# Two steps of a product-key expert layer put in another order: VectorE's step in V begins with the next tile's weights, ScalarE's step in U with the high part two tiles on

## The chip, the core and the metric

The kernel runs on one core of one Trainium2 chip. The metric is the time of one execution on the device in microseconds (us). Three executions before the change gave 3698.55, 3700.45 and 3706.06 us; their median is 3700.45 us.

## What is computed

The reference is a trunk of two layers for 512 tokens of width 1024, all in float32. Each layer has a gated mixer (attention and a convolution) and then an expert retrieval, which alone the change touches. Cut to that part:

```
q = (xt @ w_query).reshape(T, 8, 2, 128)
s = einsum('thpd,hpnd->thpn', q, sub_keys)      # scores against 2 x 128 half keys
... top 16 of each half, top 16 of their sums: ids, gates = softmax(top_s)
a    = gelu(einsum('chkd,cd->chk', u_tab[idc], xc))   # u_e . x of each chosen expert
coef = gc * a
y    = einsum('chk,chkd->cd', coef, v_tab[idc])       # sum of coef * v_e
```

There are 128 x 128 = 16384 experts in each layer, and `u_tab` and `v_tab` have a row of 1024 for each.

## The kernel before

The kernel doesn't gather the experts' rows for 384 of the 512 tokens. It multiplies the whole tables on TensorE, and weights the result with a matrix that is zero where an expert was not chosen. Only the first 128 tokens get their rows one by one: GpSimd gathers 128 rows of 4 KB at a time (`gbuf`, four buffers), and VectorE multiplies them.

**Tiles.** All matrices come as one stream of 340 tiles for each layer, each 128 x 1024 float32 (512 KB), into four slots, `raw[:, i % 4]`. The stages in order are the mixer's projections (tiles 0 to 67), the queries (68 to 83), **U** (tiles 84 to 211, the table `u`) and **V** (212 to 339, the table `v`). SyncE's queue loads tile i + 4 into a slot when TensorE has finished tile i (`load`, which waits for `tile_done`).

**The split.** Each tile is used as three products. In U and V the steps to make them ready are:
- `high_at` (U) and `high_in` (V), on ScalarE: the high part `w_hi` from `raw` (lines 1000 and 1007, "HI" below). It waits for the load alone.
- `u_low` (U, line 1715) and `weight_low` (V, line 1934), on VectorE: the 16-bit remainder `w16[.., 0]`, from `raw` and `w_hi` ("WL"). It is written into the slot of `raw`.
- `half_word`, on ScalarE (line 1012, "HW"): the 16-bit copy of the high part, `w16[.., 1]`. It is written over the rest of `raw`, so that it waits for WL of its tile.

**TensorE in a tile.** `product16` (U) and `experts` (V) first wait for HI and run 8 float32 products (lines 667 and 924), then wait for HW and run 16 products of 16-bit operands (lines 670, 671, 927 and 928).

**U, the other work.** After tile u ScalarE applies gelu to the bank (line 1256) and stores the 384 columns to `g_scr`. Between tiles 33 and 117, 48 groups build the gates' matrix: VectorE makes `one_j`, `one_i`, `gated_hi` and `gated_lo` (lines 1894 to 1899), TensorE multiplies them (lines 895 and 897, `c_group`), ScalarE copies the result to `stage` (line 1288), and SyncE's queue stores it to `c_scr`. VectorE's `dot` (line 1740) takes a gathered row block in between. The order on ScalarE in one U tile is HW(u+1), HI(u+2), gelu(u).

**V, the other work.** The right-hand side of tile k is made by `mix(k)` on VectorE (lines 1921 and 1922, "MX", from `cg`, which SyncE's queue loads from the two scratch arrays), `coef_high(k)` on ScalarE (lines 1264 and 1265, "CH"), and `mixed_low(k)` on VectorE (line 1928, "ML"), which waits for CH. `weigh(k)` (line 1913, "WG") adds one gathered row block of `v` to `y_sp`, and lets GpSimd gather the next. TensorE waits for ML(k) and HI(k) before tile k. ScalarE runs, in one V tile, CH(k+1), HW(k+1), HI(k+2). Every eighth step VectorE also takes a row of the next conditioning product (`w_row`, line 1354). VectorE's loop has 32 steps in one turn, with 3 turns and 32 further steps written out; TensorE's and ScalarE's have 4 tiles in one turn.

The waits are written by hand as semaphore counts, and each engine runs its instructions in the order of the program.

Of the kernel before, what the change touches and what calls it, by code (L numbers as in the profile page):

```python
# [79 lines left out]
I_U = 84  # L80
# [91 lines left out]
def build_trunk(nc, stream, u_rows, ada, params_d, keys_d, con_d, x_d, c_d, pos_d, c_scr, g_scr, out_d):  # L172
    with ExitStack() as ctx:
# [792 lines left out]
        def _(act):  # L966
# [25 lines left out]
            with act.Fori(0, DEPTH) as l:  # L992
                def read_no(i):

                    return l * (NE // 2) + i // 2 + 2

                def high_at(i):
                    act.wait_ge(loaded[i % 4], (l * (NT // 4) + i // 4 + 1) * 16)
                    if I_QRY <= i < NT:
                        nc.scalar.mul(w_hi[:, i % 4], raw[:, i % 4], W_UP).then_inc(hi_done, 1)  # L1000
                    else:
                        nc.scalar.copy(w_hi[:, i % 4], raw[:, i % 4]).then_inc(hi_done, 1)
# [6 lines left out]
                def half_word(s, g):  # L1009

                    act.wait_ge(lo_done, g + 5)
                    nc.scalar.mul(w16[:, s, 1], w_hi[:, s].bitcast(F32), X_DOWN).then_inc(w16_done, 1)  # L1012

                def half_word_at(i):

                    half_word(i % 4, l * NT + i)
# [66 lines left out]
                for i in range(I_Q + C):  # L1083
# [10 lines left out]
                    else:  # L1094
                        k = i - I_K if i < I_V else i - I_Q + 2
# [152 lines left out]

                def u_tile(u):

                    half_word_at(I_U + u + 1)
                    high_at(I_U + u + 2)
                    b = u % 2
                    act.wait_ge(g_st[b], (l * (NKEYS // 2) + u // 2) * 16 + 16)
                    act.wait_ge(tile_done, l * NT + I_U + u + 5)
                    nc.scalar.activation(g_out[:, b], ps[:, b, 0:ND], ACT.Gelu).then_inc(bank_read[b], 1)
                    act.wait_ge(bank_read[b], read_no(I_U + u))
                    act.dma_start(g_scr[u], g_out[:, b]).then_inc(g_st[b], 16)
# [8 lines left out]
                u = 0  # L1267
                while u < EXP_TILE:
                    u_tile(u)
                    u += 1  # L1270
                act.wait_ge(g_exp, 2 * l + 1)
                nc.scalar.activation(t16[:], t16[:], ACT.Exp).then_inc(g_exp, 1)
                while u < U_ROUTE:
                    u_tile(u)
                    u += 1
                g = 0
                while u < NKEYS:
                    if u == NKEYS - 1:
                        coef_high(0, 0)
                    u_tile(u)  # L1280
                    while g < GROUPS and group_tile(g) == u:
                        hb = g // HALF_GROUPS
                        if g % HALF_GROUPS == 0:
                            act.wait_ge(c_st, (l * STORED + max(hb - 1, 0)) * 16 * PARTS + 64)
                        for q in range(2):
                            n, tok = 2 * g + q, (GROUP * g + 4 * q) % HALF
                            act.wait_ge(c_mm, l * 2 * GROUPS + n + 5)
                            nc.scalar.mul(stage[:, hb % 2, :, tok:tok + 4].rearrange("i j t -> i t j"),
                                          ps[:, 2 + n % 4].rearrange("i (t j) -> i t j", t=4), X_UP / GATE_UP).then_inc(c_ev, 1)
                        g += 1  # L1290
                        if g == GROUPS:
                            nc.scalar.copy(st[:, 0, 4], st[:, 0, 3]).then_inc(cg_free, 4)
                    u += 1
# [26 lines left out]
        def _(dve):  # L1320
# [85 lines left out]
            with dve.Fori(0, DEPTH) as l:  # L1406
# [501 lines left out]
                def weigh(k, r):  # L1908

                    at_k = dve.snap(4 * r + k)  # L1910
                    dve.wait_ge(row_in[k % 4], (l * (2 * P // SLOTS) + P // SLOTS + r + k // 4 + 1) * 16)
                    dve.wait_ge(row_used, l * 2 * P + P + 4 * r + k + 4)
                    nc.vector.scalar_tensor_tensor(out=y_sp[:], in0=gbuf[:, k % 4], scalar=a_sp[:, bass.ds(at_k, 1)],  # L1913
                                                   in1=y_sp[:], op0=ALU.mult, op1=ALU.add).then_inc(row_used, 1)

                def mix(k, r):

                    dve.wait_ge(cf_ready, l * NKEYS + 4 * r + k + 3)
                    dve.wait_ge(cg_in[k % 4], (l * (NKEYS // 4) + r + k // 4) * 32 + 32)
                    j = dve.snap(4 * r + k)  # L1920
                    nc.vector.tensor_tensor(coef[:, k % 2, 0:NS], cg[:, k % 4, 0:NS], cg[:, k % 4, NS:2 * NS], ALU.mult)
                    nc.vector.tensor_tensor(coef[:, k % 2, NS:].rearrange("i (b t) -> i b t", b=2), stage[:, :, bass.ds(j, 1)].rearrange("i b o t -> i (b o) t"),
                                            cg[:, k % 4, 2 * NS:].rearrange("i (b t) -> i b t", b=2), ALU.mult).then_inc(cg_free, 1)

                def mixed_low(k, r):

                    dve.wait_ge(cf_hid, l * NKEYS + 4 * r + k + 1)
                    nc.vector.scalar_tensor_tensor(out=cf16[k % 4][:, 0], in0=cf_hi[k % 4][:].bitcast(F32), scalar=-1.0 / X_DOWN,  # L1928
                                                   in1=coef[:, k % 2], op0=ALU.mult, op1=ALU.add).then_inc(cf_ready, 1)

                def weight_low(k, r):

                    dve.wait_ge(hi_done, l * NT + I_W + 4 * r + k + 1)
                    nc.vector.scalar_tensor_tensor(out=w16[:, k % 4, 0], in0=raw[:, k % 4], scalar=W_UP,  # L1934
                                                   in1=w_hi[:, k % 4].bitcast(F32), op0=ALU.mult,
                                                   op1=ALU.subtract).then_inc(lo_done, 1)

                def w_step(k, r, left=2):

                    if left >= 2:  # L1940
                        mix(k + 2, r)
                    weigh(k, r)
                    if left >= 1:
                        mixed_low(k + 1, r)
                        weight_low(k + 1, r)

                mix(0, 0)
                mix(1, 0)
# [22 lines left out]
                with dve.Fori(0, 3) as r:  # L1971
                    for k in range(32):
                        w_step(k, 8 * r)
                        if k % 8 == 5:
                            w_row(k // 8, r)
                    w_rows_kept(r)
                for k in range(32):
                    w_step(k, 24, 31 - k)
                    if k % 8 == 5:
                        w_row(k // 8, 3)  # L1980
# [81 lines left out]
```

## Time and profile before

| | before |
|---|---|
| three executions | 3698.55, 3700.45, 3706.06 us |
| the profiled execution | 3699.43 us |
| its span | 3697.6 us |
| TensorE matmul busy | 3378.1 us (91%) |
| VectorE busy | 2995.0 us (81%) |
| ScalarE busy | 2179.2 us (59%) |
| GpSimd busy | 1029.0 us (28%) |
| moved by DMA | 868.89 MB, mean 235 GB/s |

The span is what the profile covers from the first to the last instruction; the execution is 1.8 us longer. V takes about 1255 to 1843 us in the first layer and 3095 to 3685 us in the second, U about 640 to 1250 and 2480 to 3090 us. A busy share says how long an engine held an instruction, not whether it set the pace; for that the waits and the timeline are read.

### The profile page before, as it was taken

The numbers are of one execution on the slowest core, as the hardware profiler recorded it, in microseconds if no ns is written. First come the engines' busy times: TensorE is split into PE (matmuls) and PEld (weight loads), VectorE is DVE, ScalarE is ACT, GpSimd is POOL, SyncE is SP. The second block draws the span as 40 slices with busy tenths as digits, with TensorE's granted clock in tenths as the row PEclk, the third lists the DMA queues.
The fourth block names the chain that finished last, engine by engine and source line by source line (L and its number), as shares of the span: only waits on it lengthen the run. The fifth ranks groups of instructions, "written<-read, shape, count | busy, mean of one in ns | idle before, by whom it ended". The sixth has DMA issues, their size and how long they took to land.

```text
span 3697.6 us, 63120 instructions
## 1 busy us (share of the span) xinstructions
PE 3378.1 (91%) x19278; PEld 2439.2 (66%) x19278; DVE 2995.0 (81%) x6039; ACT 2179.2 (59%) x3118; POOL 1029.0 (28%) x1126
## 2 busy tenths in 40 slices
PE   6999999989999998899989999999899988988998
PEld 5767766666666666666677677666666666666665
DVE  6999769987788677777769997799877786777777
ACT  4573445566776565566646724455677765655666
POOL 0000036035555322222200000550445552222221
PEclk9999999999999999999999999999999999999999
DMA  5312353579998999999822124435799989999997
GB/s 194 98 58 80 127 203 112 188 233 327 332 351 297 328 320 298 304 311 311 283 80 87 58 86 166 170 122 192 258 331 340 340 294 337 309 308 296 318 307 246
DMA packets 421669, 868.89 MB, mean 235 GB/s; under 512 B 167824, under 2 KB 233360, under 8 KB 421008
## 3 DMA queue, kind: packets, MB, share of 16 engines
q1 hardware_dynamic: 310512, 544.87, 43.8%
q0 software_dynamic: 73728, 268.47, 21.6%
q10 hardware_dynamic: 37152, 52.45, 3.8%
q8 instruction: 102, 1.67, 0.2%
q14 instruction: 175, 1.43, 0.1%
HBM read 774.41 MB, written 85.98 MB: 233 GB/s over the span
## 4 chain that ended last, share of the span: by engine, by line
issue 59%; POOL 14%; DVE 11%; ACT 10%; PE 3%; DMA 1%; ACTq 1%; DVEq 1%; POOLq 0%; SPq 0%
DVE w L1934 6%; POOL gbuf L586 5%; ACT w_hi L1007 5%; POOL spare L600 4%; ACT cf_hi L1265 2%; POOL raw L559 2%; ACT cf L1264 2%; POOL w L562 2%; DVE y_sp L1913 1%; DVE w_rows L1354 1%; PE ps L667 1%; DMA gbuf<-u_rows,ids_u 1%; PE ps L670 1%; PE ps L671 1%; POOL h L575 1%
## 5 line engine op out<-in xcount | busy, mean ns | idle before, releaser
L1012 ACT ACTIVATE w<-w_hi 128x1024 f16<-128x1024 f32 x544 | 574.8, 1057 | 776.8 <-DVE w L1934 472.3
L670 PE MATMUL ps<-h,w 128*128 128x384 f16 (+1 forms) x2272 | 756.6, 334 | 20.8 <-ACT w L1012 20.7
L927 PE MATMUL ps<-cf,w 128*128 128x384 f16 x2032 | 666.7, 329 | 100.3 <-ACT w L1012 100.2
L671 PE MATMUL ps<-h,w 128*128 128x384 f16 (+1 forms) x2272 | 753.3, 332 | 0.0
L928 PE MATMUL ps<-cf,w 128*128 128x384 f16 x2032 | 663.4, 327 | 0.0
L600 POOL TENSOR_TENSOR spare<-spare 128x1 f32<-128x1 f32 x504 | 218.5, 434 | 1400.0 <-DVE y_sp L1913 814.3
L667 PE MATMUL ps<-h_hi,w_hi 128*128 128x384 f32 (+1 forms) x2272 | 491.0, 358 | 0.0
L924 PE MATMUL ps<-cf_hi,w_hi 128*128 128x384 f32 x2032 | 435.4, 357 | 27.4 <-DVE cf L1928 27.0
L1715 DVE SCALAR_TENSOR_TENSOR w<-raw,w_hi 128x1024 f16<-128x1024 f32 x248 | 302.6, 1220 | 185.4 <-ACT w_hi L1000 185.2
L667 PEld LDWEIGHTS ps<-h_hi,w_hi 128*128 128x128 f32 x2272 | 396.9, 189 | 17.3 <-issue 0.2
L927 PEld LDWEIGHTS ps<-cf,w 128*128 128x128 f16 x2032 | 199.4, 98 | 295.5 <-ACT w L1012 176.1
L924 PEld LDWEIGHTS ps<-cf_hi,w_hi 128*128 128x128 f32 x2032 | 359.2, 191 | 46.9 <-issue 30.1
L670 PEld LDWEIGHTS ps<-h,w 128*128 128x128 f16 x2272 | 222.7, 98 | 214.1 <-issue 42.0
L1928 DVE SCALAR_TENSOR_TENSOR cf<-cf_hi,coef 128x384 f16<-128x384 f32 x256 | 142.8, 558 | 257.3 <-ACT cf_hi L1265 256.7
L586 POOL DMA_INDIRECT gbuf<-u_rows,ids_u x256 | 338.3, 1321 | 41.9 <-POOL spare L600 13.1
L1506 DVE SCALAR_TENSOR_TENSOR yT<-uT,lp,yT 128x512 f32<-128x512 f32 x480 | 327.4, 744 | 0.0
L1913 DVE SCALAR_TENSOR_TENSOR y_sp<-gbuf,a_sp,y_sp 128x1024 f32<-128x1024 f32 x256 | 327.0, 1277 | 0.0
L671 PEld LDWEIGHTS ps<-h,w 128*128 128x128 f16 x2272 | 223.9, 99 | 140.2 <-issue 1.7
L1740 DVE CUSTOM_DVE_ANT_1 gbuf<-gbuf,h_tok 128x1024 f32<-128x1024 f32 x256 | 303.3, 1219 | 15.9 <-DMA gbuf<-u_rows,ids_u 15.7
L1000 ACT ACTIVATE w_hi<-raw 128x1024 fp32r<-128x1024 f32 x296 | 309.5, 1046 | 11.3 <-DMA raw<-stream 10.8
L1934 DVE SCALAR_TENSOR_TENSOR w<-raw,w_hi 128x1024 f16<-128x1024 f32 x256 | 311.7, 1218 | 0.0
L586 POOL DMA_INDIRECT gbuf<-stream,ids_v x256 | 273.2, 1067 | 38.8 <-issue 3.1
(286 smaller groups left out, 6152.2 us busy)
## 6 DMA issues: line engine op xcount, KB each, us to landing
raw<-stream SPq DMA_DIRECT2D x682, 512.0 KB, 5.0
gelu_scratch<-g_out ACTq DMA_DIRECT2D x256, 192.0 KB, 6.7
cg<-gelu_scratch SPq DMA_DIRECT2D x256, 192.0 KB, 5.5
c_scratch<-stage SPq DMA_DIRECT2D x128, 256.0 KB
cg<-c_scratch SPq DMA_DIRECT2D x256, 128.0 KB, 4.3
qT<-ada SPq DMA_DIRECT2D x32, 512.0 KB, 6.5
cgate<-ada SPq DMA_DIRECT2D x32, 512.0 KB, 5.7
w_rows<-ada SPq DMA_DIRECT2D x32, 512.0 KB, 7.2
```

Source lines behind the costliest of these rows:

```text
L586: nc.gpsimd.indirect_dma_start(out=gbuf[:, n % SLOTS], out_offset=None, in_=table, in_offset=bass.IndirectOffsetOnAxis(ap=ids[:, k:k + 1], ...
L600: nc.gpsimd.tensor_tensor(spare[:, 16:17], spare[:, 17:18], spare[:, 18:19], ALU.add).then_inc(room, 1)
L667: nc.tensor.matmul(ps[:, b, 0:n], w_hi[:, s, c], h_hi[:, c, t0:T], start=c == 0, stop=False)
L670: nc.tensor.matmul(ps[:, b, 0:n], w16[:, s, 0, c], h16[:, c, 1, t0:T], start=False, stop=False)
L671: mm = nc.tensor.matmul(ps[:, b, 0:n], w16[:, s, 1, c], h16[:, c, 0, t0:T], start=False, stop=c == C - 1)
L924: nc.tensor.matmul(ps[:, c, P:T], w_hi[:, s, c], cf_hi[s][:], start=first, stop=False)
L927: nc.tensor.matmul(ps[:, c, P:T], w16[:, s, 0, c], cf16[s][:, 1], start=False, stop=False)
L928: mm = nc.tensor.matmul(ps[:, c, P:T], w16[:, s, 1, c], cf16[s][:, 0], start=False, stop=False)
L1012: nc.scalar.mul(w16[:, s, 1], w_hi[:, s].bitcast(F32), X_DOWN).then_inc(w16_done, 1)
L1506: ins = nc.vector.scalar_tensor_tensor(out=yT[:, c], in0=uT[:, c, k:k + T], scalar=weight, in1=yT[:, c], op0=ALU.mult, op1=ALU.add)
L1913: nc.vector.scalar_tensor_tensor(out=y_sp[:], in0=gbuf[:, k % 4], scalar=a_sp[:, bass.ds(at_k, 1)], in1=y_sp[:], op0=ALU.mult, op1=ALU.add ...
L1934: nc.vector.scalar_tensor_tensor(out=w16[:, k % 4, 0], in0=raw[:, k % 4], scalar=W_UP, in1=w_hi[:, k % 4].bitcast(F32), op0=ALU.mult, op1= ...
```

## The change

In U, ScalarE takes HI(u+2) first and HW(u+1) behind it. In V, VectorE's step k ran MX(k+2), WG(k), ML(k+1), WL(k+1); now it runs WL(k+1), ML(k+1), MX(k+2), WG(k). No instruction is added or removed, and no wait's count is changed.

```
                 def u_tile(u):

+                    high_at(I_U + u + 2)
                     half_word_at(I_U + u + 1)
-                    high_at(I_U + u + 2)
                     b = u % 2
...
                 def w_step(k, r, left=2):

+                    if left >= 1:
+                        weight_low(k + 1, r)
+                        mixed_low(k + 1, r)
                     if left >= 2:
                         mix(k + 2, r)
                     weigh(k, r)
-                    if left >= 1:
-                        mixed_low(k + 1, r)
-                        weight_low(k + 1, r)
```

## Rows read from the trace of the kernel before

**Rows 1.** Waits of the whole run: engine, line, waited for: us, times, longest

```profile
ACT w L1012 <- DVE w L1934: 472.3, 256, 6.3
...
DVE cf L1928 <- ACT cf_hi L1265: 256.7, 220, 3.3
DVE w L1715 <- ACT w_hi L1000: 185.2, 98, 3.2
...
PE ps L927 <- ACT w L1012: 100.2, 236, 0.5
...
PE ps L895 <- DVE gated_lo L1899: 66.3, 61, 2.1
...
PE ps L924 <- DVE cf L1928: 27.0, 8, 4.5
...
PE ps L670 <- ACT w L1012: 20.7, 25, 2.4
...
ACT w_hi L1000 <- DMA raw<-stream: 10.8, 14, 1.6
```

**Rows 2.** Timeline, one tile of V: start us, us, engine line op [idle before]

```profile
1504.20 0.42 DVE L1921 TENSOR_TENSOR coef<-cg 128x256 f32<-128x256 f32 x1
1504.32 1.06 ACT L1012 ACTIVATE w<-w_hi 128x1024 f16<-128x1024 f32 x1 [1.76 <-DVE w L1934]
...
1504.54 0.28 DVE L1922 TENSOR_TENSOR coef<-stage,cg 128x128 f32<-128x128 f32 x1
1504.74 1.28 DVE L1913 SCALAR_TENSOR_TENSOR y_sp<-gbuf,a_sp,y_sp 128x1024 f32<-128x1024 f32 x1
...
1505.28 1.04 ACT L1007 ACTIVATE w_hi<-raw 128x1024 fp32r<-128x1024 f32 x1
...
1505.43 0.34 PE L927 MATMUL ps<-cf,w 128*128 128x384 f16 x1 [0.42 <-ACT w L1012]
...
1506.23 0.51 ACT L1264 ACTIVATE cf<-coef 128x384 f16<-128x384 f32 x1
...
1506.64 0.51 ACT L1265 ACTIVATE cf_hi<-coef 128x384 fp32r<-128x384 f32 x1
...
1507.18 0.56 DVE L1928 SCALAR_TENSOR_TENSOR cf<-cf_hi,coef 128x384 f16<-128x384 f32 x1 [1.16 <-ACT cf_hi L1265]
...
1507.66 1.22 DVE L1934 SCALAR_TENSOR_TENSOR w<-raw,w_hi 128x1024 f16<-128x1024 f32 x1
...
1507.91 1.69 PE L924 MATMUL ps<-cf_hi,w_hi 128*128 128x384 f32 x8
...
1508.91 1.06 ACT L1012 ACTIVATE w<-w_hi 128x1024 f16<-128x1024 f32 x1 [1.76 <-DVE w L1934]
```

**Rows 3.** Timeline of TensorE in V just after VectorE's loop turned

```profile
1573.88 1.69 PE L924 MATMUL ps<-cf_hi,w_hi 128*128 128x384 f32 x8
...
1577.88 1.69 PE L924 MATMUL ps<-cf_hi,w_hi 128*128 128x384 f32 x8
```

**Rows 4.** DMA issues of the page: KB each, median us from issue to landing

```profile
raw<-stream SPq DMA_DIRECT2D x682, 512.0 KB, 5.0
```

**Rows 5.** Windows: busy us of each engine, TensorE clock, DMA share, GB/s

```profile
1000.00:1060.00 60.00, 57.01 (x407) 40.88 (x404) 49.64 (x74) 45.02 (x52) 29.90 (x30) 1.00 0.99 349
...
1417.00:1550.00 133.00, 121.59 (x699) 84.39 (x698) 102.68 (x152) 82.08 (x116) 37.61 (x59) 0.99 0.94 306
...
3100.00:3220.00 120.00, 108.94 (x629) 75.50 (x629) 93.19 (x139) 73.91 (x105) 33.27 (x52) 1.00 0.97 326
```

**Rows 6.** Timeline of VectorE where its loop turns in V

```profile
1413.61 0.42 DVE L1921 TENSOR_TENSOR coef<-cg 128x256 f32<-128x256 f32 x1 [5.41 <-issue]
```

**Rows 7.** Timeline of ScalarE in U, one tile

```profile
807.99 1.06 ACT L1012 ACTIVATE w<-w_hi 128x1024 f16<-128x1024 f32 x1 [1.76 <-DVE w L1715]
808.95 1.04 ACT L1000 ACTIVATE w_hi<-raw 128x1024 fp32r<-128x1024 f32 x1
```

**Rows 8.** Timeline of VectorE in U, the same place

```profile
810.03 1.23 DVE L1715 SCALAR_TENSOR_TENSOR w<-raw,w_hi 128x1024 f16<-128x1024 f32 x1 [2.07 <-ACT w_hi L1000]
```

## The prediction, made before the changed kernel was run

> **What bounds the kernel now.** I read the waits first. Two of ScalarE's and VectorE's waits stand out, and they face each other: HW in V waits 472.3 us for WL, in 256 of 256 tiles, and ML waits 256.7 us for CH, which is ScalarE's [rows 1]. Two engines that wait for each other in every tile are a ring, whatever their busy shares. So the next view is the timeline of one V tile, and the reader should follow it as a circle [rows 2]. HW starts at 1504.32, HI 0.96 us later, the first half of CH 0.95 later, the second 0.41 later; ML starts 0.54 later, WL 0.48 later, and 1.25 after that, at 1508.91, the next HW. The sum is 0.96 + 0.95 + 0.41 + 0.54 + 0.48 + 1.25 = 4.59 us. That is the whole period: nothing in it is a wait for TensorE or a DMA. TensorE's first 16-bit product waits for HW [rows 2], 236 times in V [rows 1].
>
> How fast TensorE would be alone is seen where it had a backlog, behind a turn of VectorE's loop: there the tiles start 4.00 us apart [rows 3]. So 0.59 us of each 4.59 is the ring's. The 0.42 us that the waits show (100.2 us in all [rows 1]) understates it, since the ends of matmuls are modelled.
>
> In U the chain is another. ScalarE's HW waits for WL, HI stands behind HW, and VectorE's next WL waits for HI: 2.07 us at 810.03 [rows 8], 98 times and 185.2 us in all [rows 1]. The gates' operands come behind that WL, and TensorE waits for them 61 times, 66.3 us, and for HW 25 times, 20.7 us [rows 1]. That is 87 us in both layers.
>
> **V, part by part.** Nothing is added. The VectorE operations of a step keep their durations: from start to start 0.48 (ML), 0.34 and 0.20 (MX), and WL and WG last 1.22 and 1.28 [rows 2], together 3.52 us. ScalarE's four take 0.96 + 0.95 + 0.41 + 0.51 = 2.83 us. Both are below TensorE's 4.00, also with a conditioning row every eighth step. What changes is who waits. WL(k+1) no longer stands behind ML(k+1), so not behind CH(k+1) either. It needs HI(k+1) alone, which ScalarE finished in the step before. The ring is cut, and three shorter ones are left:
> - WL, HW, HI of the next tile, WL: 1.25 + 0.96 + 1.07 = 3.28 us for a tile.
> - CH, ML, MX of the next tile, CH: 0.92 + 0.03 + 0.48 + 0.34 + 0.31 = 2.08 us.
> - HI, WL, ML, MX, WG, WL, HW, HI over two tiles: 1.07 + 1.22 + 0.48 + 0.54 + 1.28 + 1.25 + 0.96 = 6.80 us, 3.4 for one.
>
> ML(k+1) behind WL(k+1) costs nothing: CH takes 0.92 us after HI, WL 1.25, so CH is done first. Moved back are MX(k+2) and WG(k). MX has SyncE's queue behind it, which loads the coefficients for four tiles on and then waits for TensorE's tile anyway; WG has GpSimd behind it, whose gather is wanted four tiles later. Their cover is the four buffers, 4 x 4 us against a landing of 5.0 us for a load of the stream [rows 4]. If that cover went, each would cost its lateness once in a tile. The raw slots have the same cover: from the end of tile k to the start of k+4 are three tiles, 12 us, for the landing and HI.
>
> So something else bounds the tile: TensorE at 4.00, or the DMA engines. They are busy 0.94 of V at 306 GB/s, 0.97 at 326 in the fuller stretch [rows 5]. A tile moves 306 x 4.59 = 1.41 MB. Estimates of its least time: if packets keep their lengths and the share can reach the 0.99 seen in U, 4.59 x 0.94 / 0.99 = 4.36 us. If V can have U's 349 GB/s [rows 5], 1.41 MB take 4.03 us. The packets get shorter under load, as the rows show: 306 / 0.94 is 326 GB/s for a full share, 326 / 0.97 is 336, and U's 349 / 0.99 is 353. I take V's own fuller stretch, 336 GB/s, and get 1.41 / 336 = 4.20 us, since U moves fewer short pieces and is the farther row. The gain is 0.39 us in each of the 236 tiles that waited [rows 1]: 92 us. The ends are 0.23 x 236 = 54 and 0.59 x 236 = 139.
>
> At this place a page of the Trainium skill says more, and my sum doesn't use it. "DMA: Bandwidth & Descriptors", section "Where 436 GB/s comes from", puts the limit from HBM at about 358 GB/s for a core. By that rule 1.41 MB would take 3.94 us, TensorE would be the bound, and the gain would be the 139 us end. The trace agrees so far as no window of these rows is above it (349), but V's share is nearly full at 306 to 326.
>
> **The turns of the loop.** VectorE stands 5.41 us at a turn for its instructions [rows 6]; TensorE waits for ML 8 times, 27.0 us in all, at the turns and at V's start [rows 1]. After the change VectorE can be ahead when it stops: it needs only HI, thus the load, which lands about a tile before its need. I take 8 of the 27 us; the ends are 0, if the DMAs take up the lead, and 27.
>
> **U.** HI(u+2) goes ahead of HW(u+1). At 807.99 ScalarE had been idle for 1.76 us when HW began, and HI came at 808.95 [rows 7]: HI could begin up to 2.7 us earlier if its load has landed, and VectorE's 2.07 us of waiting [rows 8] go, with the group's operands behind. HW(u+1) comes up to 1 us later, where ScalarE isn't idle; it is covered by TensorE's tile in hand, as HW is made a tile ahead. Behind it are gelu(u), its store and the group's copy, each of which waits for TensorE's tile u. Not covered is a late load: HW(u+1) now waits for the load of tile u+2, and ends up to 1.04 + 1.06 = 2.1 us after it lands [rows 7]. That happens where HI waits for its load today, 14 times in U and the queries, 10.8 us [rows 1], so at most 14 x 2.1 = 29 us lost. The ends for U are thus 29 us lost and 87 gained. I take 30 gained: half of the 87, since part of those waits is VectorE's own work in tiles with a group each and part a late load, less half of the 29.
>
> **The sum.** 92 + 8 + 30 = 130 us. The profiled execution took 3699.4 us (span 3697.6 and 1.8 around it), so 3569.4; the median of the runs is 1.0 above it. I predict 3570 us.
>
> **Rivals, and their chances.**
> - My forecast, DMA engines and TensorE nearly level, 3530 to 3610: 0.42.
> - The DMA engines bound V by their time, 4.36 us for a tile. For it: a share of 0.94 to 0.97 [rows 5]. Against: packets that shorten under load. 54 us in V, none at the turns, 15 in U: 3631. Chance 0.18.
> - TensorE bounds V at 4.00. For it: four tiles' cover, and U's 349 GB/s. 139 + 16 + 40 = 195 us: 3504. Chance 0.17. This is also where the page's 358 GB/s would lead.
> - V as forecast, but U loses, because faster tiles make loads late and HW is held behind HI in as many places as today's 14: 100 - 29 = 71 us, 3629. Chance 0.12.
> - The change doesn't do in V what it says: another ring of the same length closes, for example CH(k+1) behind HI(k+1) with ML and MX behind it, or a gather that lands late because WG moved back. Against it stand the three sums above, the longest 3.4 us. Only U's 30 us stay: 3669. Chance 0.07.
> - Slower: in U ScalarE is held at loads in most tiles, 2.1 us each. It decides from 100 / 2.1 = 48 of the 256 U tiles on; at 96 tiles the time is 3699 - 100 + 202 = 3801. For it: U's share of 0.99 in the densest window. Against: 14 late loads now. Chance 0.04.
>
> About 0.2% (7 us) is what a measurement of this kernel can tell from no change. Faster by more than that are all but the last two cases and most of the last but one, 0.93; 0.03 within, where V keeps its pace and U gives nothing; 0.04 slower. The range that leaves out no more than 2 in 10 reaches from the TensorE case to just past the DMA case: 3500 to 3645.
>
> **What would show it.** ML's wait for CH and HW's wait for WL in V nearly gone; the order on VectorE WL, ML, MX, WG, and HW no longer 0.03 us behind WL. Tile starts of line 924 about 4.2 us apart instead of 4.59; if 4.0, TensorE bounds, and if 4.36 or uneven, with HI waiting for `raw`, the DMA engines do. The DMA share in V at 0.97 or more and 336 GB/s. In U, WL's wait for HI well below 185 us, the wait for `gated_lo` about halved, and some new waits of line 670 for HW behind HI's wait for a load. My prediction is wrong above all if V's packets don't shorten, or if they shorten as in U.

## The result, and the profile after

The changed kernel took 3491.93 us (median of 4, 3484.96 to 3496.24), beside 3700.9 us before: a ratio of 0.9432, 95% interval 0.941 to 0.9453. That is 209 us less, where 130 were forecast, and below the range of 3500 to 3645. The direction, the ring and the place of the gain were right. The size was not: the case that the prediction gave 0.17 came in, TensorE as the bound of V (3504), with more from U on top.

Where the time went is read from the starts of TensorE's tiles in the two profiled executions, whose spans differ by 203 us (3697.6 and 3494.4). From the first to the last tile of V it took 1194.0 us in both layers together before and 1040.8 after, 153 less. From the first to the last tile of U it was 1228.4 and 1177.6, 51 less. (The first layer's V before reaches to 1858.6 us, not to 1843 as said above.)

First the waits of the changed kernel, whole run (engine, line, waited for: us, times, longest). They answer to [rows 1].

```profile
ACT w L1012 <- DVE w L1934: 174.5, 254, 5.5
ACT w_hi L1007 <- DMA raw<-stream: 125.2, 114, 3.7
DVE w L1934 <- ACT w_hi L1007: 113.6, 106, 3.3
...
ACT w_hi L1000 <- DMA raw<-stream: 105.5, 96, 3.5
...
DVE w L1715 <- ACT w_hi L1000: 97.3, 60, 4.5
...
PE ps L670 <- ACT w L1012: 40.0, 36, 3.1
...
PE ps L924 <- DVE cf L1928: 23.6, 9, 4.3
...
DVE cf L1928 <- ACT cf_hi L1265: 6.3, 2, 3.2
```

The two lines that closed the ring are changed: HW's wait for WL fell from 472.3 to 174.5 us, and ML's for CH from 256.7 us, 220 times, to 6.3 us, 2 times. TensorE's wait for HW in V (line 927, 100.2 us before) is gone. In its place a wait appears that V did not have: HI waits for its load, 114 times. In U and the queries the same wait went from 14 times to 96. ScalarE now stands at the loads, which costs nothing as long as TensorE has a tile in hand. One sign that the prediction named did not come: HW still waits for WL 254 times, and starts 0.03 us behind its end in the tile shown next, since ScalarE gets to HW before WL has ended. That wait no longer sets the period.

One tile of V on the timeline (start us, us, engine, line), to be laid beside [rows 2]:

```profile
1444.23 1.69 PE L924 MATMUL ps<-cf_hi,w_hi 128*128 128x384 f32 x8
1444.50 1.06 ACT L1007 ACTIVATE w_hi<-raw 128x1024 fp32r<-128x1024 f32 x1 [1.32 <-DMA raw<-stream]
1445.47 0.51 ACT L1264 ACTIVATE cf<-coef 128x384 f16<-128x384 f32 x1
1445.59 1.23 DVE L1934 SCALAR_TENSOR_TENSOR w<-raw,w_hi 128x1024 f16<-128x1024 f32 x1 [1.30 <-ACT w_hi L1007]
1445.88 0.51 ACT L1265 ACTIVATE cf_hi<-coef 128x384 fp32r<-128x384 f32 x1
1446.73 0.55 DVE L1928 SCALAR_TENSOR_TENSOR cf<-cf_hi,coef 128x384 f16<-128x384 f32 x1
1446.85 1.06 ACT L1012 ACTIVATE w<-w_hi 128x1024 f16<-128x1024 f32 x1 [0.47 <-DVE w L1934]
1447.20 0.42 DVE L1921 TENSOR_TENSOR coef<-cg 128x256 f32<-128x256 f32 x1
...
1448.23 1.69 PE L924 MATMUL ps<-cf_hi,w_hi 128*128 128x384 f32 x8
```

TensorE's tiles start 4.00 us apart (1444.23 and 1448.23), the pace that it showed only in its catch-up before [rows 3]. The next steps in V are 4.01 us for the most part. WL and CH now run side by side, WL on VectorE and CH on ScalarE, both from HI on; ML and HW follow at once. HW for the next tile ends at 1447.91, and TensorE's first product that needs it starts at 1449.76, about 1.5 us after the tile's start.

The windows of V (busy us of PE, PEld, DVE, ACT, POOL, then TensorE's clock, DMA share, GB/s):

```profile
1280.00:1350.00 70.00, 70.00 (x423) 50.11 (x420) 61.71 (x93) 50.11 (x69) 42.54 (x35) 1.00 1.04 365
1400.00:1470.00 70.00, 70.00 (x420) 50.38 (x419) 61.67 (x93) 51.54 (x72) 42.95 (x36) 1.00 1.05 360
1640.00:1740.00 100.00, 100.00 (x601) 71.80 (x600) 86.91 (x131) 71.71 (x100) 59.51 (x52) 1.00 1.02 347
```

Against [rows 5]: TensorE is busy 70.00 of 70 us at the full granted clock (2.4 GHz), and the DMAs move 347 to 365 GB/s; the two windows of V shown there had 306 and 326, and the same three stretches of the kernel before had 315, 298 and 319. The DMA share is 1.02 to 1.05: it is a sum of packets' times over 16 engines, and passes 1 here.

U, the groups' stretch of the first layer, waits of the changed kernel from 770 to 1240 us:

```profile
DVE w L1715 <- ACT w_hi L1000: 50.8, 30, 4.5
ACT w_hi L1000 <- DMA raw<-stream: 48.8, 45, 3.4
...
PE ps L670 <- ACT w L1012: 11.7, 10, 3.1
...
PEld ps L895 <- issue: 5.1, 10, 1.1
...
PE ps L895 <- DVE gated_lo L1899: 1.8, 3, 0.7
```

and the same lines and stretch of the kernel before:

```profile
DVE w L1715 <- ACT w_hi L1000: 88.1, 44, 3.1
PEld ps L895 <- issue: 49.2, 46, 2.5
PE ps L895 <- DVE gated_lo L1899: 32.4, 29, 2.1
...
ACT w_hi L1000 <- DMA raw<-stream: 3.1, 5, 0.9
PE ps L670 <- ACT w L1012: 2.0, 3, 0.9
```

TensorE's wait for the gates' operands went from 32.4 to 1.8 us, and the weight loads' idle time ahead of them from 49.2 to 5.1. Its wait for HW rose from 2.0 to 11.7: that is the cost of HW behind HI, and it is real but small. How much this makes for a tile is in the section on the prediction.

### The profile page after: what moved, and what is told of

It is laid out like the page before. It is cut to its first block, busy times and chain, and to the rows that moved or that the text cites. A ratio compares the mean times of both kernels' runs of the same rounds, so it can differ in the third digit from the quotient of the medians.

```text
span 3494.4 us, 63120 instructions
## 1 busy us (share of the span) xinstructions
PE 3328.6 (95%) x19278; PEld 2443.3 (70%) x19278; DVE 2984.3 (85%) x6039; ACT 2191.8 (63%) x3118; POOL 1330.3 (38%) x1126
## 4 chain that ended last, share of the span: by engine, by line
PE 40%; issue 26%; DVE 15%; POOL 10%; DMA 4%; ACT 3%; DVEq 0%; POOLq 0%; SPq 0%; ACTq 0%
PE ps L924 9%; PE ps L927 8%; PE ps L928 8%; POOL gbuf L586 6%; POOL spare L600 5%; PE ps L636 4%; PE ps L638 3%; PE ps L637 3%; DVE yT L1506 3%; DVE i L1752 2%; DMA raw<-stream 2%; DVE v L1748 1%; DVE S_ring L1758 1%; DMA gbuf<-u_rows,ids_u 1%; PE ps L670 1%
## 5 line engine op out<-in xcount | busy, mean ns | idle before, releaser
L1012 ACT ACTIVATE w<-w_hi 128x1024 f16<-128x1024 f32 x544 | 572.5, 1052 | 286.3 <-DVE w L1934 174.5
L600 POOL TENSOR_TENSOR spare<-spare 128x1 f32<-128x1 f32 x504 | 393.9, 782 | 909.2 <-DVE a_sp L1740 500.9
L924 PE MATMUL ps<-cf_hi,w_hi 128*128 128x384 f32 x2032 | 430.6, 354 | 23.6 <-DVE cf L1928 23.6
L1000 ACT ACTIVATE w_hi<-raw 128x1024 fp32r<-128x1024 f32 x296 | 313.7, 1060 | 144.6 <-DMA raw<-stream 105.5
L586 POOL DMA_INDIRECT gbuf<-stream,ids_v x256 | 383.3, 1497 | 38.3 <-POOL spare L600 2.6
L586 POOL DMA_INDIRECT gbuf<-u_rows,ids_u x256 | 352.7, 1378 | 40.9 <-POOL spare L600 9.5
L570 POOL TENSOR_TENSOR spare<-spare 128x1 f32<-128x1 f32 x2 | 0.4, 193 | 926.9 <-DVE w_lo L1411 926.9
L1007 ACT ACTIVATE w_hi<-raw 128x1024 fp32r<-128x1024 f32 x248 | 260.5, 1050 | 126.2 <-DMA raw<-stream 125.2
```

Source lines behind the costliest of these rows:

```text
L586: nc.gpsimd.indirect_dma_start(out=gbuf[:, n % SLOTS], out_offset=None, in_=table, in_offset=bass.IndirectOffsetOnAxis(ap=ids[:, k:k + 1], ...
L600: nc.gpsimd.tensor_tensor(spare[:, 16:17], spare[:, 17:18], spare[:, 18:19], ALU.add).then_inc(room, 1)
L924: nc.tensor.matmul(ps[:, c, P:T], w_hi[:, s, c], cf_hi[s][:], start=first, stop=False)
```

## The experiments

All ratios are to the kernel before, run on the same chip beside the changed one. Where a V order is tried in experiments 3 and 4, U has its new order.

**1. V's new order alone.** The edit is the second part of the diff; U is as before.

> V's new order alone, U as before. My theory after the result: the two parts are independent; in V the ring of 4.59 us is cut and TensorE's 4.01 us bounds each tile, about 146 us for both layers by the starts of the tiles, so about 3549 us. Rival: the U part also sets up V (DMAs further ahead at V's start), then V alone gives less, 3560 us or more.

Measured: 3551.33 us (3548.68 to 3554.53), ratio 0.9586 (0.957 to 0.9602), beside 3705.16: 154 us less. By the interval V's share of the gain is thus 147 to 159 us; by the tile starts V took 154 us less than before, and U 4 us more.

**2. U's new order alone.** The first part of the diff.

> U's new order alone, V as before. My theory: 51 us of the gain are U's, so about 3650 us, and V's tiles stay 4.59 us apart. Rival (my forecast's size): 30 us, 3670 us. Rival: HW held behind late loads takes the gain back, 3690 us or more.

Measured: 3638.61 us (3635.9 to 3646.66), ratio 0.9826 (0.9808 to 0.9844): 66.5 us less, 58 to 71 by the interval; by the tile starts U took 62 us less, and V the same as before. The expectation of 51 us was what the changed kernel's first profile showed in U; its repeat in experiment 9 shows 60, so U varies by some 10 us between executions. 30 and "taken back" are both refuted. The product of the two ratios is 0.9419, within the interval of the whole change, so the parts don't need each other.

**3. Only the last two change places.** WL ahead of ML, but both behind MX and WG.

```
                 def w_step(k, r, left=2):

                    if left >= 2:
                        mix(k + 2, r)
                    weigh(k, r)
                    if left >= 1:
-                        mixed_low(k + 1, r)
                         weight_low(k + 1, r)
+                        mixed_low(k + 1, r)
```

> The changed kernel, but V's step is MX, WG, WL, ML: of the old order only WL and ML change places, and nothing is moved ahead of MX and WG. Theory: what counts is that WL no longer stands behind ML and so behind CH; the ring is cut all the same, V's tiles 4.01 us apart, 3492 us within 10. Rival: WL must begin the step, since 1.8 us of MX and WG ahead of it make HW late; then tiles at 4.2 or more and 3540 us or more.

Measured: 3480.2 us (3474.85 to 3484.27), ratio 0.9397 (0.9381 to 0.9413), 2 us below the range expected. V's steps are 4.01 us and the rival of 3540 us is refuted: the whole of V's gain is in this one exchange.

**4. The pair first, ML still ahead of WL.**

```
                     if left >= 1:
-                        weight_low(k + 1, r)
                         mixed_low(k + 1, r)
+                        weight_low(k + 1, r)
                     if left >= 2:
                         mix(k + 2, r)
                     weigh(k, r)
```

> The changed kernel, but V's step is ML, WL, MX, WG: the pair begins the step, as in the change, but ML stays ahead of WL. Theory: the ring HW, HI, CH, ML, WL, HW is closed as before, each tile takes 4.59 us again, and only U's gain is left: 3640 to 3650 us. Rival: the gain is from taking the pair ahead of MX and WG; then 3500 us.

Measured: 3629.58 us (3626.64 to 3629.82), ratio 0.9794 (0.9778 to 0.981), 10 us below the range expected. The time is U's gain and 9 us more than in experiment 2. Those 9 us are mostly at the turns of VectorE's loop in V: TensorE's four steps from tile to tile over a turn took 8.46 to 9.45 us in experiment 2 and take 6.81 to 7.20 here, and V is 7.5 us shorter. The timeline of VectorE and ScalarE in V:

```profile
1450.00 1.06 ACT L1012 ACTIVATE w<-w_hi 128x1024 f16<-128x1024 f32 x1 [1.76 <-DVE w L1934]
...
1452.86 0.56 DVE L1928 SCALAR_TENSOR_TENSOR cf<-cf_hi,coef 128x384 f16<-128x384 f32 x1 [1.17 <-ACT cf_hi L1265]
1453.34 1.22 DVE L1934 SCALAR_TENSOR_TENSOR w<-raw,w_hi 128x1024 f16<-128x1024 f32 x1
...
1454.59 1.06 ACT L1012 ACTIVATE w<-w_hi 128x1024 f16<-128x1024 f32 x1 [1.76 <-DVE w L1934]
```

From HW to HW 4.59 us, with the same two waits as in [rows 2], 1.76 and 1.17. Taking the pair to the head of the step does nothing for the tile, and is worth some 8 us at the turns; putting WL ahead of ML is what cuts the ring. Experiments 3 and 4 together show it.

**5. The kernel before with less for TensorE.** In 127 of the 128 V tiles of a layer 8 of 24 products are left out (the last tile has lines of its own; the expectations say 125), so the output lacks them.

```
                     for c in W_ORDER:
-                        nc.tensor.matmul(ps[:, c, P:T], w16[:, s, 0, c], cf16[s][:, 1], start=False, stop=False)
                         mm = nc.tensor.matmul(ps[:, c, P:T], w16[:, s, 1, c], cf16[s][:, 0], start=False, stop=False)
```

> The kernel before with the same 8 products of a V tile left out. Theory: the ring of ScalarE and VectorE sets the tile, so its 4.59 us stay although TensorE has 1.3 us less to do, and the time stays within 10 us of before. Rival: TensorE is part of the pace; then tiles fall below 4.4 us and the kernel gains 50 us or more.

Measured: 3703.12 us, one run, beside 3703.72. Some 330 us less work for TensorE (8 products of 0.16 us in 254 tiles) changed nothing. Its timeline of TensorE:

```profile
1451.28 1.66 PE L924 MATMUL ps<-cf_hi,w_hi 128*128 128x384 f32 x8 [0.97 <-DVE cf L1927]
...
1455.87 1.66 PE L924 MATMUL ps<-cf_hi,w_hi 128*128 128x384 f32 x8 [0.97 <-DVE cf L1927]
```

The tiles are still 4.59 us apart, now with a wait of 0.97 us ahead of them.

**6. The changed kernel with the same products left out.** The same edit.

> The changed kernel with 8 of the 24 products of a V tile left out (the 8 of the 16-bit remainder with cf16[.., 1]; 125 of 128 tiles). Its output lacks them. TensorE's tile falls from 4.01 to 2.7 us, so that what comes next is seen. Theory: the DMA engines can do more than my forecast gave them; the tile comes down to VectorE's own 3.4 to 3.6 us, with 390 GB/s or more. Rival: DMAs stood just below the surface at the 352 to 362 GB/s of the changed kernel; then tiles stay at 3.9 to 4.0 us.

Measured: 3451.64 us, one run: 28 to 40 us below the changed kernel's two medians (3479 and 3492), of the same 330 us. So something stands close beneath TensorE. From 1280 to 1350 us 18 tiles are loaded, 3.9 us each, at 373 GB/s (the third window behind experiment 8), and VectorE is busy 61.91 of 70 us. The starts of the tiles tell the two apart. Of the 254 steps 127 are at most 3.45 us, most of them 3.34 us, which is VectorE's own step (3.35 us from one WL to the next behind the turn shown below). The others are longer: 4.48 us where VectorE takes a conditioning row as well, and up to 5.7 us elsewhere (7.9 at the turns); the mean is 3.96 us. ScalarE waits for loads there, 78 times and 93.0 us in V. So VectorE sets about half of these tiles, and late loads are what is seen to wait in the rest.

**7 and 8. The changed kernel with more bytes.** Behind each load of V from the fifth tile on, a half (7) or a quarter (8) of the next tile is loaded once more, to a place that nobody reads. The edit for a half, without the buffers and semaphores that it needs:

```
                         load(k % 4, l * NT + I_W + 32 * r + k + 4)
+                        if k >= 4 or k0 == 0:
+                            n = sp.snap(l * NT + I_W + 32 * r + k + 4)
+                            sp.wait_ge(more_in[k % 4], (l * 30 + 8 * r + k // 4) * 16)
+                            sp.dma_start(more[k % 4][:], stream[n][:, 0:C // 2]).then_inc(more_in[k % 4], 16)
```

> The changed kernel with 256 KB more loaded beside each V tile from the fifth on (a half of the next tile once more, into a free place that nobody reads). A tile then moves 1.67 MB instead of 1.41. Theory: the limit of the DMA engines is near 390 GB/s, so tiles of 4.2 to 4.3 us, 50 to 70 us more than the changed kernel. Rival 1 (my forecast's 336 to 353 GB/s hold for long): 4.7 to 5.0 us. Rival 2 (the limit is above 415 GB/s): the tile stays 4.01 us.

> As with 256 KB more beside each V tile, but 128 KB. The two runs before put the limit of the DMA engines in V at 364 to 372 GB/s, whatever the tile held. Theory: a tile of 1.573 MB then takes 4.2 to 4.3 us where the conditioning rows are loaded, and 1.507 MB 4.05 to 4.15 us in the last quarter; 3530 to 3550 us in all. Rival: there is no fixed limit, a tile slows with each added transfer in proportion (0.7 us for 256 KB), so 4.35 us in all quarters.

Measured: 3614.56 us with 256 KB and 3538.07 us with 128 KB, one run each. The larger one is 0.49 us a tile more than the changed kernel (118 us between the profiled spans of 3612.7 and 3494.4, over about 240 tiles), not the 0.2 to 0.3 expected, nor the 0.7 to 1.0 of the forecast's rates. With that limit known, the smaller one came within its range, and its tiles roughly too: from quarter to quarter of V, without the first two steps of each, 4.24, 4.24, 4.28 and 4.11 us in the first layer, 4.37, 4.32, 4.22 and 4.15 in the second; the last quarter has no conditioning rows. The rival, 4.35 us in all quarters, doesn't fit. The windows from 1280 to 1350 us, in this order: with 256 KB, with 128 KB, and the changed kernel with fewer products:

```profile
1280.00:1350.00 70.00, 62.98 (x366) 43.30 (x365) 55.67 (x84) 45.89 (x64) 26.60 (x30) 1.00 1.06 376
```

```profile
1280.00:1350.00 70.00, 67.52 (x396) 46.60 (x394) 55.26 (x83) 45.88 (x64) 27.56 (x32) 1.00 1.07 372
```

```profile
1280.00:1350.00 70.00, 54.40 (x279) 36.83 (x277) 61.91 (x93) 50.80 (x71) 43.68 (x37) 0.95 1.07 373
```

Three kernels with different tiles end at the same 372 to 376 GB/s. (In the last quarter of V, from 1640 to 1700 us, it is 358, 370 and 365.) And in the one with 256 KB more the waits of this window are:

```profile
ACT w_hi L1014 <- DMA raw<-stream: 18.7, 12, 3.4
...
PE ps L931 <- DVE cf L1938: 7.0, 7, 2.5
```

HI waits for loads again (line 1014 there), and now TensorE waits too, which in the changed kernel it did not. That is what a bound by DMA looks like here, about 373 GB/s in V. Whether the DMA engines or the memory behind them set it, no run here shows. It holds for V's mix of transfers alone: in U the changed kernel moved more for 12 us,

```profile
1036.00:1048.00 12.00, 10.11 (x70) 7.23 (x68) 7.34 (x12) 6.48 (x8) 6.94 (x8) 1.00 1.03 389
```

**9 and 10. The changed kernel again, beside the order of experiment 3.**

> The changed kernel once more, beside the next one on the same chip: 3480 to 3496 us, ratio about 0.943 to before.

> The order MX, WG, WL, ML in V once more. Its first run was 0.9397 of before, the changed kernel's 0.9432. Theory: both stand at TensorE's 4.01 us in V and have the same U, so within 0.2% of each other here. Rival: MX and WG early let the transfers behind them start early, which is worth 5 to 12 us.

Measured, five executions each: the change 3479.09 us (3472.91 to 3481.09), ratio 0.938 (0.9366 to 0.9394); the order MX, WG, WL, ML 3486.98 us (3481.89 to 3489.03), ratio 0.9401 (0.9388 to 0.9414). The lead of experiment 3 over the first measurement of the change did not hold. Here the change is ahead by 8 us, 0.2%, there it was behind, and the intervals overlap; neither order is shown to be the better. The expectation for the change itself, 0.943, was missed by half a per cent: its ratio moved by as much from one measurement to the other.

## Why the prediction was wrong, step by step

- **The ring.** Right. 0.96 + 0.95 + 0.41 + 0.54 + 0.48 + 1.25 is the period of 4.59 us, TensorE has no part in it (experiment 5), and WL ahead of ML cuts it (3 and 4). It held for nearly all of V's tiles, not only for the 236 that the prediction counted by TensorE's waits: 227 of the 254 steps from tile to tile are 4.59 us before, and 237 are 4.01 after.
- **TensorE's own pace, 4.00 us, taken from two rows behind a turn** [rows 3]. Right: 1444.23 to 1448.23 after.
- **The least time of a V tile by DMA. This is the step that failed.** I divided 1.41 MB by V's own fuller stretch, 336 GB/s, and got 4.20 us. The 336 was worked out as 326 GB/s over a share of 0.97, with a share of 1.00 for the ceiling [rows 5]. Both halves were wrong. The share is no ceiling at 1.00 (1.02 to 1.07 in these runs), and the rate under demand is 372 to 376 GB/s (7, 8). A tile of 512 + 512 + 192 + 128 KB and an eighth of 512 KB, 1.44 MB, takes 1.44 / 0.373 = 3.87 us by that, below TensorE's 4.00. So V gained the whole 0.58 us in each of its 254 steps, 147 us, and some 6 us more at its start, its end and the turns: 153 us by the tile starts, 147 to 159 by experiment 1, where the sum took 0.39 x 236 = 92 and 8. The far end that stood in the text, 0.59 x 236 = 139, was nearer, and short by the count.
- **The rule on the limit of a core, in the Trainium skill's page "DMA: Bandwidth & Descriptors", section "Where 436 GB/s comes from".** It led to the right bound, TensorE, but its 358 GB/s is not the limit here: 365 in the changed kernel and 376 in experiment 7 are above it. That section works its figure out as a stack's 716 GB/s over two cores, and one core runs here; no run shows what a second one would take.
- **The turns of the loop, 8 us.** About right. TensorE's waits for ML fell from 27.0 to 23.6 us only. But the four steps over a turn went from 8.35 to 9.09 us down to 6.01 to 7.15, and what the turns cost beyond the steady pace, the catch-up behind them counted, fell from 16.6 to 11.2 us (7.3 in experiment 9). VectorE still stands at a turn, with nothing in the profile that it waits for, now ahead of WL:

```profile
1370.14 1.23 DVE L1934 SCALAR_TENSOR_TENSOR w<-raw,w_hi 128x1024 f16<-128x1024 f32 x1 [3.62 <-issue]
...
1373.49 1.22 DVE L1934 SCALAR_TENSOR_TENSOR w<-raw,w_hi 128x1024 f16<-128x1024 f32 x1
```

  3.62 us instead of 5.41 [rows 6], and the two tiles of TensorE around it start 6.01 us apart:

```profile
1365.96 1.69 PE L924 MATMUL ps<-cf_hi,w_hi 128*128 128x384 f32 x8
1371.97 1.66 PE L924 MATMUL ps<-cf_hi,w_hi 128*128 128x384 f32 x8 [1.71 <-DVE cf L1928]
```

- **U, 30 us. The second term that was mis-sized.** Right in its mechanism, off by about two in its size: 51 and 60 us by the tile starts of the changed kernel, 62 in experiment 2. I halved the 87 us of waits for VectorE's own work and for late loads, and took 14 off for HW held behind loads. Neither deduction was due in that size. The whole gain is in the 96 tiles that have a group: 568.7 us before, 518.8 in the changed kernel, 506.1 in experiment 2, while the other 158 steps took 659.8, 658.8 and 660.4 us. Two starts of line 667, with a group between them, before:

```profile
788.31 1.64 PE L667 MATMUL ps<-h_hi,w_hi 128*128 128x384 f32 x8
...
793.24 0.23 PE L895 MATMUL ps<-gated_hi,one_i 128*128 128x128 f16 x1 [0.68 <-DVE gated_lo L1899]
...
794.14 1.64 PE L667 MATMUL ps<-h_hi,w_hi 128*128 128x384 f32 x8
```

  and after:

```profile
785.95 1.65 PE L667 MATMUL ps<-h_hi,w_hi 128*128 128x384 f32 x8
...
790.94 1.65 PE L667 MATMUL ps<-h_hi,w_hi 128*128 128x384 f32 x8
```

  That is 5.83 and 4.99 us, in the second of two neighbouring tiles with a group each. A tile of U without a group takes about 4.0 us, and a group's 16 products about 0.9, so the 4.99 are TensorE's own work: VectorE's own work kept next to nothing of the gain. In the groups' stretch of the first layer the waits for operands fell by 30.6 us of 32.4, and those for HW rose by 9.7. The loads were late far more often than the 14 times that I bounded the loss with (96), but TensorE has a tile in hand when HI waits, and of the whole run's waits for HW only 19.3 us were added (20.7 to 40.0). Where they come, they are costly: in one place of U TensorE stood for 3.15 us, and its products then started 0.32 us apart instead of 0.16 for some 3 us, with a granted clock of 0.50, the level of 1.2 GHz:

```profile
1049.67 0.34 PE L670 MATMUL ps<-h,w 128*128 128x384 f16 x1 [3.15 <-ACT w L1012]
...
1050.93 0.53 PE L670 MATMUL ps<-h,w 128*128 128x384 f16 x1
```

```profile
1050.60:1053.40 2.80, 2.80 (x10) 1.37 (x9) 2.80 (x6) 2.00 (x2) 0.00 (x0) 0.50 0.40 151
```

- **The waits as a measure of U's gain.** They were too small a one: those counted, 66.3 + 20.7 before, less 4.2 + 32.3 in experiment 2, are 50.5 us, and the tiles show 62. The ends of matmuls are modelled, so a wait begins too late in the profile. In the tile that begins at 788.31 the row of line 895 shows a wait of 0.68 us, and the tile is 0.84 us longer than the same one after. V's 0.42 shown and 0.58 gained is the same thing, which the prediction allowed for in V and not in U.
- **The slower case** needed 48 tiles of U held; TensorE waited for HW 36 times, 11 more than before, about a microsecond each.

## What to carry to other kernels

When two engines wait for each other once in every tile, add up the start-to-start times around the circle: if they make the period, a faster third engine or a faster transfer doesn't help, and one exchange that takes an operation from behind a wait that it doesn't need can be worth the whole gap to the next bound. Look for that bound by a measured rate under demand, in bytes per tile and GB/s; a busy share near 1 of a resource whose transfers overlap is no proof that it is full. And a wait that moves from an engine's critical place to a load with a tile in hand is not a cost until the tile in hand is used up, however often it is counted. The sum of waits for a matmul is too low where ends are modelled; the distance from tile to tile is the safer number.

## What the runs showed that was not expected

- The DMA share of the records passes 1.00: 1.04 at 365 GB/s, 1.07 at 372 GB/s.
- The transfers held 372 to 376 GB/s in V's mix of 4 KB, 1.5 KB and 256 B packets (and of 2 KB or 1 KB for the extra loads), and 389 for 12 us in U. The changed kernel's 360 to 365 are within 4% of 373, so that V is nearly level between TensorE and DMA: dropping a third of the products gains only 28 to 40 us.
- The same pair of kernels gave 0.9432 (0.941 to 0.9453) in one measurement and 0.938 (0.9366 to 0.9394) in another; about half of the 19 us between the two profiled spans is in U. Differences of half a per cent between measurements are not to be read here.
